# Banded attention heads scored two at a time, with the scaling of the weights and low halves of weight tiles on GpSimd

## The reference

```python
def second_block(x, c, ...):
    ...
    h = rmsnorm_2(x, norm_g) * (1.0 + scale) + shift
    sb_q, sb_k, sb_v, sb_g, sw_q, sw_k, sw_v, sw_g = split(h @ w_in)
    y_sb = stick_breaking_attention(sb_q, sb_k, sb_v) * silu(sb_g)     # 8 heads of 64
    y_sw = sliding_window_sink_attention(sw_q, sw_k, sw_v, sinks, slopes) * silu(sw_g)
    x = x + gate * (concat([y_sb, y_sw]) @ w_out)
    return rmsnorm_2(x, final_g)

def sliding_window_sink_attention(q, k, v, sinks, slopes):   # 8 query heads of 64, 2 key/value heads
    # a block of 128 queries sees its own 128 keys and the 128 before them
    s = einsum(q, k) * 64 ** -0.5
    logits = where(valid, s - m * rel, -1e30)       # m: slope of the head, rel: distance
    p = softmax(concat([logits, sink]))[..., :-1]   # one learned sink logit per head
    return einsum(p, v)
```

## Time and profile before

| | us |
|---|---|
| runs of the kernel (median of 3; lowest, highest) | 1706.58; 1706.09, 1708.05 |
| profiled execution, its own time | 1703.44 |
| its span, first to last instruction | 1701.70 |
| PE busy | 1680.1 |
| DVE busy | 1064.3 |
| ACT busy | 707.0 |
| POOL busy | 23.9 |

### The profile page before, as it was taken

One profiled execution on the slowest core, in us unless ns is written; L12 is line 12 of the kernel. 1 busy time (PEld: TensorE's weight loads), 2 busy tenths in 40 slices (PEclk: granted clock), 3 DMA queues, 4 the chain that ended last, 5 costly groups with the idle time before them and its releaser, 6 DMA issues.

```text
span 1701.7 us, 21153 instructions
## 1 busy us (share of the span) xinstructions
PE 1680.1 (99%) x8045; PEld 1373.6 (81%) x8045; DVE 1064.3 (63%) x1513; ACT 707.0 (42%) x1138; POOL 23.9 (1%) x42
## 2 busy tenths in 40 slices
PE   8999999999999999999999999999999999999998
PEld 7888888888888888886668888888888888977776
DVE  5799763565555533488875456555555867367695
ACT  7213543453333322345764264333332113166674
POOL 1000000000000000011100000000000000000000
PEclk9999999999999999999999999999999999999999
DMA  6272422123222232311104303332327642320201
GB/s 209 79 232 86 159 89 75 53 97 99 98 92 89 94 108 93 94 61 41 50 4 146 99 26 99 99 99 99 99 96 237 192 142 70 104 81 26 75 26 50
DMA packets 154294, 164.40 MB, mean 97 GB/s; under 512 B 2998, under 2 KB 150383, under 8 KB 153967
## 3 DMA queue, kind: packets, MB, share of 16 engines
q1 hardware_dynamic: 153408, 162.51, 29.5%
q0 software_dynamic: 336, 0.53, 0.2%
q10 hardware_dynamic: 479, 0.39, 0.1%
HBM read 160.01 MB, written 3.15 MB: 96 GB/s over the span
## 4 chain that ended last, share of the span: by engine, by line
PE 91%; DVE 5%; ACT 3%; issue 1%; DMA 1%; SPq 0%; DVEq 0%; ACTq 0%
PE bank L928 89%; ACT xa_p L1674 1%; PE bank L1373 1%; DMA x_nat<-in_x_dram 1%; DVE w_lo L2188 1%; DVE nmax L2694 0%; DVE mla_pT_b L2706 0%; DVE h_lo L2188 0%; ACT mla_p L1674 0%; ACT w_hi L1674 0%; PE bank L1633 0%; PE bank L1660 0%; DVE xa_pT_lo L2188 0%; DVE mla_q L2655 0%; PE bank L998 0%
## 5 line engine op out<-in xcount | busy, mean ns | idle before, releaser
L928 PE MATMUL bank<-h_hi,w_hi 128*128 128x512 f32 x1472 | 579.0, 393 | 3.0 <-DVE w_lo L2188 1.5
L928 PE MATMUL bank<-h_hi,w_lo 128*128 128x512 f32 x1472 | 573.3, 389 | 0.0
L928 PE MATMUL bank<-h_lo,w_hi 128*128 128x512 f32 x1472 | 573.0, 389 | 0.0
L2188 DVE TENSOR_TENSOR w_lo<-w_raw,w_hi 128x2048 fp32r<-128x2048 f32 (+4 forms) x142 | 286.1, 2019 | 232.3 <-ACT w_hi L1674 232.0
L1674 ACT ACTIVATE w_hi<-w_raw 128x2048 fp32r<-128x2048 f32 (+4 forms) x142 | 239.2, 1690 | 382.7 <-PE bank L928 377.2
L928 PEld LDWEIGHTS bank<-h_hi,w_hi 128*128 128x128 f32 x1472 | 276.1, 188 | 67.6 <-issue 7.2
L928 PEld LDWEIGHTS bank<-h_hi,w_lo 128*128 128x128 f32 x1472 | 276.1, 188 | 58.2
L928 PEld LDWEIGHTS bank<-h_lo,w_hi 128*128 128x128 f32 x1472 | 276.2, 188 | 57.7 <-issue 1.2
L928 PE MATMUL bank<-g_hi,w_hi 128*128 128x512 f32 x352 | 137.5, 391 | 0.0
L928 PE MATMUL bank<-g_hi,w_lo 128*128 128x512 f32 x352 | 137.0, 389 | 0.0
L928 PE MATMUL bank<-g_lo,w_hi 128*128 128x512 f32 x352 | 137.0, 389 | 0.0
(11 more groups left out here) (374 smaller groups left out, 2060.8 us busy)
## 6 DMA issues: line engine op xcount, KB each, us to landing
w_raw<-in_ffn_w_up_dram SPq DMA_DIRECT2D x44, 1024.0 KB, 5.0
w_raw<-in_ffn_w_down_dram SPq DMA_DIRECT2D x16, 1024.0 KB, 5.2
w_raw<-in_w_in_dram SPq DMA_DIRECT2D x13, 1024.0 KB, 5.3
w_whole<-in_xa_wkv_dram SPq DMA_DIRECT2D x12, 1024.0 KB, 5.4
ada_w<-in_w_ada_dram SPq DMA_DIRECT2D x12, 1024.0 KB, 7.8
w_raw<-in_xa_wq_dram SPq DMA_DIRECT2D x8, 1024.0 KB, 5.2
w_raw<-in_xa_wo_dram SPq DMA_DIRECT2D x8, 1024.0 KB, 5.1
w_raw<-in_pc_w_in_dram SPq DMA_DIRECT2D x6, 1024.0 KB, 5.3
```

The source lines that it names most:

```text
L928: return nc.tensor.matmul(o, w, v, start=start, stop=stop, **kw)
L2188: return tt(lo_, v, hi.bitcast(f32), SUB)
```

## The change

The diff outside this stage only lets semaphores share names. Inside it:

- Scores are issued per pair of heads. For each query block the even head's matmul (partitions 0 to 63) is followed by the odd head's (64 to 127), in another bank. `w_place` gives each head of a pair two banks of its own.
- `relm` times the slope is made on ACT (`sw_rel`), and one DVE instruction adds it to the scores, flips the sign and takes the smallest over the row, with the negated sink as the start. So the separate reduction and the comparison with the sink are gone. Such an instruction is two entries in the queue: the operation and a read of the accumulator into `nmax`.
- `sw_p` has four buffers instead of two and a 257th column with the sink, so that the exponential's own sum holds the sink; `esink` and its addition are gone.
- Multiplication by `rinv` moves from ACT to POOL (two instructions per head: 128x128 and 128x3x256).
- Low halves of all 12 weight quarters move from DVE to POOL. Slab 3 is in quarters too. On ACT the quarters' high halves stand behind the exponentials of a pair. The low halves of the outputs (`h_lo`) stay on DVE.
- PE's tiles 8 to 15 are issued in other parts, and each has a bank of its own.

```diff
-        wp = put("sw_p", [P, 2, NB, 2 * P])
+        wp = put("sw_p", [P, 4, NB, 2 * P + 1])
+        rel_h = put("sw_rel", [P, 2, 2 * P])
...
+        def w_place(h, b):
+            return bank[4 + 2 * (h % 2) + b]
...
         def out_bank(u):
-            return bank[(0, 1, 2, 4)[u % 4] if u >= 8 else (u + 1) % 3]
+            return bank[(0, 1, 2, 4, 5, 6, 7, 3)[u - 8] if u >= 8 else (u + 1) % 3]
@@ POOL @@
+            def low_quarter(part):
...
+                m = nc.gpsimd.tensor_tensor(w_lo[k][:, c], raw[k][:, c], w_hi[k][:, c].bitcast(f32), SUB)
+            def window_scale(h):
+                pool.wait_ge(wrinv_ready, h + 1)
+                v, r = wp[:, h % 4, :, :], rinv[:, h % 2, :].rearrange("p (a o) -> p a o", o=1)
+                nc.gpsimd.tensor_tensor(v[:, 0, P:2 * P], v[:, 0, P:2 * P], rinv[:, h % 2, 0:1].broadcast_to([P, P]), MUL)\
+                    .then_inc(wp_ready, 1)
+                nc.gpsimd.tensor_tensor(v[:, 1:, 0:2 * P], v[:, 1:, 0:2 * P],
+                                        r[:, 1:, :].broadcast_to([P, NB - 1, 2 * P]), MUL)\
+                    .then_inc(wp_ready, 1)
+            for pair, (ahead, behind) in enumerate((((0, 1), ()), ((2, 3), ()), ((), (4, 5)), ((6,), (7, 8, 9, 10, 11)))):
+                for part in ahead:
+                    low_quarter(part)
+                for h in (2 * pair, 2 * pair + 1):
+                    window_scale(h)
+                    if h + 4 < SWH:
+                        window_sink(h + 4)
+                for part in behind:
+                    low_quarter(part)
@@ PE @@
-            for h in range(SWH):
-                window_scores(h)
-                if h >= 3 and h % 2:
-                    window_values((h - 3) // 2)
-                out_part(h, 0, 4, so_lo if h == 0 else None)
-                if h:
-                    window_turn(h - 1)
+            for pair in range(SWH // 2):
+                window_scores(pair)
+                if pair >= 2:
+                    window_values(pair - 2)
+                if pair:
+                    window_turn(2 * pair - 2)
+                out_part(2 * pair, 0, 4, so_lo if pair == 0 else None)
+                if pair:
+                    window_turn(2 * pair - 1)
+                out_part(2 * pair + 1, 0, 4, None)
@@ ACT @@
+            for pair, behind in enumerate(((3,), (), (4, 5, 6), (7, 8, 9, 10, 11))):
+                window_exp(2 * pair)
+                window_exp(2 * pair + 1)
+                if pair >= 2:
+                    window_hi(pair - 2)
+                if pair < SWH // 2 - 1:
+                    window_rel(2 * pair + 2)
+                    window_rel(2 * pair + 3)
+                for part in behind:
+                    output_quarter(part)
@@ DVE @@
-                        stt(wp[:, h % 2, q, c0:], relm[:, c0:], -slope, b[:, (q % 2) * 2 * P + c0:(q % 2 + 1) * 2 * P],
-                            MUL, ADD).then_inc(wl_done, 1)
-                    link(nc.vector.tensor_reduce(nmax[:, h % 2, :], wp[:, h % 2, :, :], AX.X, MAX))
-                    ts(nmax[:, h % 2, :], nmax[:, h % 2, :], sinks[:, h:h + 1], -1.0, MAX, MUL).then_inc(wmax_done, 1)
+                    nc.vector.tensor_tensor_reduce(
+                        out=wp[:, h % 4, q, c0:2 * P], in0=w_place(h, q // 2)[:, q % 2 * 2 * P + c0:(q % 2 + 1) * 2 * P],
+                        in1=rel_h[:, h % 2, c0:], scale=-1.0, scalar=sinks[:, h:h + 1], op0=ADD, op1=ALU.min,
+                        accum_out=nmax[:, h % 2, q:q + 1]).then_inc(wl_done, 1)
...
+            for pair in range(SWH // 2):
+                window_logits(2 * pair)
+                window_logits(2 * pair + 1)
+                if pair >= 2:
+                    window_gate(pair - 2)
+                window_sums(2 * pair)
+                if pair == 1:
+                    add_out(0)
+                if pair:
+                    turned_copy(2 * pair - 2)
+                    add_out(2 * pair - 1)
+                window_sums(2 * pair + 1)
+                if pair:
+                    turned_copy(2 * pair - 1)
+                    if pair >= 2:
+                        window_low(pair - 2)
+                    add_out(2 * pair)
```

More of the change, by code:

```diff
@@ new lines, in window_rel, with window_exp @@
+            def window_rel(h):
+                wait(act, wl_done, 4 * (h - 1))
+                a(rel_h[:, h % 2, :], relm[:, :], ACT.Copy, scale=-2.0 ** (-8.0 * (h + 1) / SWH)).then_inc(rel_ready, 1)
+            def window_exp(h):
+                act.wait_ge(sink_set, h + 2)
+                for q in range(NB):
+                    act.wait_ge(wl_done, 4 * h + q + 1)
+                    v = wp[:, h % 4, q, P if q == 0 else 0:]
+                    a(v, v, ACT.Exp, bias=nmax[:, h % 2, q:q + 1], scale=-1.0,
+                      accum_out=rsum[:, h % 2, q:q + 1]).then_inc(wexp_done, 1)
@@ L2161, in _ @@
+            window_hi(SWH // 2 - 2)
+            window_hi(SWH // 2 - 1)
             for i in range(DT):
@@ L2167, in _ @@
             act.wait_ge(stat2_done, 4)
-            a(kv_col[:, :], bank[7][:, 0:NB], ACT.Sqrt, scale=1.0 / D, bias=eps[:, :]).then_inc(col_sqrt, 1)
-            act.wait_ge(col_ready, 1)
+            a(kv_col[:, :], bank[7][:, 0:NB], ACT.Sqrt, scale=1.0 / D, bias=eps[:, :]).then_inc(col_step, 1)
+            act.wait_ge(col_step, 2)
             for t in range(NB):
@@ L2883, in _ @@
                     tt(o, stick_out(h), o, MUL).then_inc(so_scaled, 1)
-            for b in range(2):
-                link(nc.vector.memset(wp[:, b, 0, 0:P], NEG))
             dve.wait_ge(gate_act, 8)
@@ new lines, in window_sums, with turned_copy @@
+            def window_sums(h):
+                dve.wait_ge(wexp_done, 4 * h + 4)
+                wait(dve, wp_ready, 2 * (h - 1) if h >= 2 else 0)
+                nc.vector.reciprocal(rinv[:, h % 2, :], rsum[:, h % 2, :]).then_inc(wrinv_ready, 1)
+            def turned_copy(e):
+                flat = wpT[:, e % 2, :, :].rearrange("p a n -> p (a n)")
+                for b in range(2):
+                    dve.wait_ge(wt_ready, 2 * e + b + 1)
+                    wait(dve, wo_ready, e // 2)
+                    n = 4 * P - b * P
+                    cp(flat[:, b * 512:b * 512 + n], w_place(e, b)[:, 0:n]).then_inc(wt_done, 1)
@@ new lines, in window_gate, with window_low @@
+            def window_gate(pair):
+                dve.wait_ge(wo_ready, pair + 1)
+                wait(dve, wo_lo, pair - 1)
+                tt(fb[pair % 2][:, :], bank[3][:, :], wg_T[:, pair, :], MUL).then_inc(wo_scaled, 1)
+            def window_low(pair):
+                dve.wait_ge(wo_hi, pair + 1)
+                low(h_lo[:, 4 + pair, :], fb[pair % 2][:, :], h_hi[:, 4 + pair, :]).then_inc(wo_lo, 1)
+            dve.wait_ge(sink_set, 1)
+            for pair in range(SWH // 2):
[4 more added lines that the diff above has]
+                window_sums(2 * pair)
+                if pair == 1:
+                    add_out(0)
[8 more added lines that the diff above has]
+                    add_out(2 * pair)
```

255 lines of the change are left out of this document (117 added, 138 removed).

## The result

The changed kernel took 1691.28 us (median of 4 runs, 1690.73 to 1692.23) against 1706.34 (4 runs, 1703.52 to 1708.05) for the kernel before: a ratio of 0.9921, 95% interval 0.9908 to 0.9934.

The account below looks back on a forecast made before the run. The prediction took PE's own work plus its waits to bound the stage: -6.9 us for scores and -2.5 for waits give -9.4, so 1706.6 - 9.4 = 1697.2 us, range 1694.0 to 1702.0.

Parts of the forecast that it names:

- What bounds the kernel: Banded stage: time follows when PE finishes tile 15, its own work from 1612.6 us on plus its waits, 4.5 us.
- Scores: PE's score matmuls: a pair of heads takes 1.72 us, as one head did, so four pairs save 6.9 us.
- Tiles, transposes and value matmuls are the same number: PE's other work in the stage: taken as unchanged, so only the scores change PE's work.
- Waits of 2.0 remaining: PE's waits: 1.25 plus 0.7 us left instead of 4.5, none at tile 12, saving 2.5 us.
- At head 0's transposes: PE's first remaining wait: 1.25 us for DVE's logits, the two halves starting at 1622.5 and 1623.3.
- Before tile 8: PE's second remaining wait: 0.7 us for slab 2's last low quarter on POOL, ready at 1651.6 against 1651.0.
- a median may lie 1 us off: Margin of the whole-run range: moved the lower end from 1695.3 us, all waits gone, to 1694.0; same margin upward.
- Contention: DVE beside POOL: only the four `h_lo` have two SBUF inputs, slowed 0.7 us each at most, with more slack.
- The fused instruction at half rate: Rival on DVE: 2.55 us per head, later scores, transposes and tile 8; gain 6.0, 1700.6 us; chance 0.13.
- GpSimd sets the pace: Rival on POOL: at 1.4 times the price tile 8 waits 5.7 us; gain 4.4, 1702.2 us; chance 0.09.
- Halves that don't overlap: Rival on PE: scores stay at 13.8 us, only waits go; -2.9, 1703.7 us; chance 0.05.
- The slower rival: POOL products at twice the price: tile 8 waits 15 us, transposes 9 more; +12.4, 1719.0 us; chance 0.06.

Follow-up runs that it names:

- e6: Changed kernel with the low halves of the weight quarters moved back from GpSimd to VectorE; stage 69.01 us, median 1694.78 us, ratio to before 0.9939.
- e7: Changed kernel with both the products by rinv back on ScalarE and the low quarters back on VectorE; stage 71.69 us, median 1695.89 us, ratio to before 0.9946.
- e5: Changed kernel with the products by rinv moved back from GpSimd to ScalarE; stage 71.29 us, median 1697.26 us, ratio to before 0.9952.
- e4: Changed kernel with both heads' transposes issued together behind a pair's first output tile; stage 66.82 us, median 1692.36 us, ratio to before 0.9939.
- e8: Changed kernel with GpSimd's products using a full tensor of gate values instead of repeated rinv; stage 65.91 us, 1690.13 us in one run.
- e12: Changed kernel with the fused instruction split into penalty add, reduction and sink minimum, without ScalarE's tables; stage 73.22 us, median 1701.23 us, ratio to before 0.9980.
- e3: Changed kernel with a pair's scores issued head by head instead of alternating; stage 67.71 us, median 1693.45 us, ratio to before 0.9937.
- e1: The kernel before, unchanged, timed again; stage 77.25 us, median 1703.74 us, ratio to before 1.0002.
- e2: The kernel before with only the changed kernel's shared semaphore names outside the stage; stage 77.25 us, median 1704.53 us, ratio to before 0.9999.
- e10: The changed kernel, unchanged, timed again; stage 65.45 us, median 1693.03 us, ratio to before 0.9932.
- e11: e3 with value matmuls placed between the two heads' scores for the last two pairs; stage 69.78 us, 1697.39 us in one run.

## Why the prediction was off

The mechanism was right, sign and places too; the size wasn't. The stage lost 11.7 us where I summed 9.4, by PE's work on the transposes and by the waits, and the median on which I put the sum was high by more than the 1 us that I allowed. Point by point:

- **What bounds the kernel: right.** PE's work and waits account for the stage in every kernel here, once the clock behind a long wait is counted.
- **Scores: right.** 1.72 us per pair; -6.8 by the timelines, where I had -6.9.
- **"Tiles, transposes and value matmuls are the same number": the step that failed in PE's work.** They are the same number and not the same time. Eight sets of transposes had cost 6.57 us together, six with scores behind (0.85 to 0.89 each) and two with a tile behind (0.68 and 0.71); without waits they cost 5.6 now, since a tile follows all. The prediction knew the price, 0.7 ahead of a tile, used it in the pace of a pair (10.5 instead of 10.9) and left it out of the sum. That is 0.9; with some 0.2 in the tiles, which I put down to fewer breaks of shape in tiles 8 to 13, PE's work fell by 8.0 and not 6.9.
- **Waits of 2.0 remaining: two terms mis-sized.** At head 0's transposes 0.5 (0.40 and the overhang of a record) and 0.3 are left, for DVE as forecast, where I had 1.25. The halves came 9.6 and some 10.3 us into the stage, not 9.9 and 10.7: the fused instruction needs 1.49 us per head and not 1.62, its accumulator read having no slot of its own. Before tile 8 nothing is left where I had 0.7: GpSimd needs 1.77 per head and not 2.27, and its last quarter was ready 0.6 before PE came. There is none at tile 12, as forecast, but e6 and e7 show that the reason wasn't the move to GpSimd. So 3.7 of 4.5 us went, not 2.5. Together: -8.0 - 3.7 = -11.7.
- **The range: "a median may lie 1 us off" was too small.** Later medians of the kernel before are 1704.25, 1704.54 and 1703.5, 2.0 to 3.1 below 1706.6. Of the 5.9 us between 1697.2 and 1691.28, 2.3 are the stage's and 3.6 lie outside it. With the measured 11.7 on 1706.6 the time would have been 1694.9, still inside the range, so it was this term that carried it out; on 1704, -11.7 gives 1692.3, beside the 1691.28 and 1693.03 measured. The lower end was the same sum with all waits gone (-11.3; its own terms give -11.4), which leaves no room for an error in PE's work.
- **Contention: the kind right, the size forecast too small.** With GpSimd on the weight quarters, the three `h_lo` took 1.69, 1.71 and 1.60 us; e6, with the quarters on VectorE, has 0.68. That is 1.0 more each, not 0.7 at most, and hidden. GpSimd's three quarters took 4.20 beside one, and 3.74 in e5.
- **The rivals.** The fused instruction at half rate: no. GpSimd sets the pace: no, it was idle from 1629.3 to 1634.1 and from 1641.8 to 1644.7; but e4, e8 and e12 show how close its chain to tile 8 is. Halves that don't overlap: no, and e3 shows that they overlap in part even ungrouped. The slower rival (+12.4) had the right place, tile 8, and left out one thing: behind waits of 3.38 us the clock fell too.

What makes whole runs of one kernel differ is on record as well, for the most part: the granted clock. The two fastest of e1's eleven executions (1701.76 and 1701.85 us) have a mean clock of 0.999, the slowest (1706.88) 0.995. In the traces, the stage begins at 1610.57 to 1611.00 us where the clock never fell ahead of it (e2, e4, e8), and at 1613.91 to 1615.06 where it fell three times (e3, e5, e6, e7, e10, e11). One of these falls lies behind the wait of 2.52 us; another lies near 1416 us in the kernel before, where PE is busy throughout (3.00 of 3.00 us in each window from 1405 to 1417). Why they come in one execution and not in another isn't shown.

## What to carry to other kernels

When an instruction's neighbours change, its slot changes: count the slots of everything on the bounding engine by what follows it, not only what is added or removed. Price a wait of TensorE in two parts, the wait and the work behind it at half clock; here two waits of 1.7 and 2.34 us cost only themselves, and those of 2.38 to 3.38 us 1.5 to 1.7 times their length. The second part is a risk and not a fixed price: behind the wait of 2.52 us it came in nine traces of 14. And judge a change inside one stage by the length of that stage, if it repeats within 0.1 us where whole runs differ by 3; read the clock of both first.

## What the runs showed of the hardware that I had not expected

- Two groups of four 64-row score matmuls on opposite row halves, issued one group behind the other, took 2.48 us, where alternated they took 1.72 and separated by other matmuls 2 x 1.71 (e3, e11).
- The same wait of TensorE of 2.52 us, with the same work behind it, was followed by a granted clock of 0.50 in nine traces and of 1.00 in five; one of 2.34 us left it at 1.00 (e12), one of 2.38 us had 0.50 behind it (e6). Executions of one kernel with a lower mean clock were the longer ones (e1: 1701.8 us at 0.999, 1706.9 at 0.995).
- On GpSimd, a product of 128x768 with an operand repeated along the row took 1.47 us, with a full one 1.64, and a difference of 128x512 1.28: 1.9, 2.1 and 2.5 ns per column, fixed part included.
- The accumulator read of VectorE's fused instruction (0.09 us) began together with the next fused instruction, so it had no slot of its own.
